# Router product on turned tokens before norm and shift, other bank pairs for two output projections, and fillers in the attentions

## Chip, cores, metric

One core of one Trainium2 chip. The metric is device time of one execution in microseconds (us), median of several.

## What is computed

256 tokens of width 1024 pass two layers and then a second block. Each layer is attention (A: forgetting attention, B: latent attention), output projection with a gate, and a grouped mixture of experts:

```python
x = x + g1[:, None, :] * mix
h = modulate(rmsnorm(x, ffn_norm_g[layer]), sh2, sc2)      # h*(1+sc2)+sh2
x = x + g2[:, None, :] * grouped_moe(h, router_w, router_bias, ...)
# in grouped_moe
scores = sigmoid(hf @ router_w)                            # 16 experts in 4 groups
g = argmax over groups of the sum of the best two (scores + bias)
# the best two experts of that group, weights normed to sum 1
```

The modulation vectors (sh1, sc1, g1, sh2, sc2, g2) come from silu(c) @ w_mod + b_mod. The second block (state space branch, sparse attention, and a product-key expert layer that gathers rows by index) follows.

## The kernel before

All engines run programs written out by hand, with semaphores between them; what stands first in an engine's list runs first. Tokens lie in C=2 chunks of P=128 partitions. PS is the partial-sum memory, 8 banks of 512 columns. TensorE works on a pair of banks for each piece of a matmul stage; `pair_of` says which, and `before[g]` is the last earlier piece on that pair, whose evacuation must be waited for.

The work around the change, in order, for layer 0 (layer 1 is the same with attention B, `b_o`, `mod1_e`):

- `attention("A")`: eight steps. TensorE computes scores two steps ahead (`scores`), VectorE masks them and takes the maximum (`mask`), ScalarE exponentiates (`exps`), VectorE divides (`norm`), TensorE turns them (`transposes`), ScalarE copies them out (`pt`), TensorE multiplies by the values (`values`), ScalarE copies (`o`). Beside it ScalarE and VectorE split the projection's weights into high and low parts (`highs`, `lows`).
- `gemm("a_o")`, the output projection, 96+96 matmuls of 512 columns in split form; VectorE adds gate times result to X (`add_product`, L2113).
- `gemm_mod("mod0_d")`: a piece of the modulation in two partial products (L952) that ScalarE copies to PARTS (L1652), then summed over partitions (`mod_total`, L961). VectorE adds it into MOD (`add_mod`, L2099).
- VectorE computes sum of squares (L2059; ScalarE does the second chunk, L1784), the inverse root by a polynomial (`inverse_root`, six small operations), then for each chunk H = X * root * GAIN (L2074), H = H + shift (L2078), where GAIN already holds norm weight times (1+scale). After each chunk `h_ready` rises.
- `experts(layer)`: TensorE issues fillers (`keep_clock`, L1072, one matmul is two records of 128 columns), turns the chunk of H (L1110) for ScalarE to copy into HT (L1611), and multiplies by the router's weights (L1116). ScalarE: sigmoid (L1711). VectorE: scores, group choice (to L2339), while H is cut into a rounded high part (L2316 on VectorE for chunk 0, L1712 on ScalarE for chunk 1) and the rest, the low part (L2310). TensorE counts group members (L1130 to L1134). VectorE derives the order of groups (`order`, L2360; SP's expert loads wait for it), and the slots as selection matrices PICKS (L2403). TensorE gathers tokens into slots (`slot_rows`, L1151: high and low part, two chunks, 8 banks: 32 matmuls of 384 columns), ScalarE copies them out (L1727), and the quads of expert matmuls begin (L1206, L1221). In layer 0, four strips (L1082) and biases (L1097) of later modulations stand between router and slot rows in TensorE's list, evacuated by ScalarE at L1718.
- SP loads expert weights in a ring of four slots (L723). POOL loads bias rows into GAIN and other accumulators (L784) after `h_ready`. ScalarE computes two Sin (L1830, L1832) before `tp("h_ffn0")`.

## Time and profile before

| | us |
|---|---|
| median of 3 runs | 1844.51 (1844.16 to 1849.18) |
| profiled execution | 1842.19 |
| its span, first to last instruction | 1840.4 |
| TensorE busy | 1668.8 (91%) |
| VectorE busy | 1013.4 (55%) |
| ScalarE busy | 637.6 (35%) |
| mean granted TensorE clock | 0.991 of full |
| HBM read | 606.21 MB, 330 GB/s over the span |

The stages: attention A from about 134 us, its projection to 193, experts of layer 0 from 227 to about 497, attention B from 613, projection to 671, experts of layer 1 from 705 to 975, then the second block, whose gather of rows by index ends the execution. Busy shares are means over stages with different limits; what counts for the change is the chain in the stretch between an output projection and the first expert quad, and at the start of each attention.

### The profile page before, as it was taken

To read this page: it belongs to the slowest core of one execution; us is meant where nothing else is said; L and a number is where in the kernel's file an instruction comes from. 1 tells how busy PE (TensorE), PEld (TensorE's weight loads), DVE (VectorE), ACT (ScalarE), POOL (GpSimd) and SP (SyncE) were. 2 spreads that over 40 slices of the span, in tenths; PEclk is the share of its full clock that TensorE was granted. 3 is DMA by queue.
4 is the path that set the end of the run, shared out by engine and by line. 5 is a ranking of instruction groups with operands and counts; after the bars stand their busy time and mean duration, and the time that the engine had idled before them with its cause. 6 is when DMAs were issued, how large, how long until landed. Compare 5 with 4: busy or idle time off the path is not lost.

```text
span 1840.4 us, 25300 instructions
## 1 busy us (share of the span) xinstructions
PE 1668.8 (91%) x9813; PEld 831.6 (45%) x9813; DVE 1013.4 (55%) x2154; ACT 637.6 (35%) x1162; POOL 303.7 (16%) x342
## 2 busy tenths in 40 slices
PE   8998999999999799999999999999899977777777
PEld 4866633323376575333336554655445533233322
DVE  4327721232473763233237985567776676767655
ACT  2336344434234633544433013322222232222222
POOL 0100000000000000000800000143334353343330
PEclk9999999999999999999999999999999999999999
DMA  9881899999856419999983434499999999999997
GB/s 360 295 301 58 338 418 352 417 416 416 345 205 235 166 46 366 414 400 388 390 329 107 160 136 161 192 425 425 424 419 419 426 427 427 426 428 427 427 427 295
DMA packets 154667, 608.92 MB, mean 331 GB/s; under 512 B 13338, under 2 KB 18626, under 8 KB 121139
## 3 DMA queue, kind: packets, MB, share of 16 engines
q1 hardware_dynamic: 114752, 327.03, 46.1%
q0 software_dynamic: 39504, 279.59, 36.3%
q8 instruction: 77, 1.26, 0.3%
q10 hardware_dynamic: 292, 0.70, 0.1%
q14 instruction: 42, 0.34, 0.0%
HBM read 606.21 MB, written 1.05 MB: 330 GB/s over the span
## 4 chain that ended last, share of the span: by engine, by line
PE 62%; DMA 24%; DVE 8%; ACT 3%; issue 2%; POOL 1%; SPq 0%; ACTq 0%; DVEq 0%; POOLq 0%
PE PS L1221 17%; DMA peer_rows<-in_peer_rows,MOD 15%; PE PS L1206 9%; PE PS L901 6%; PE PS L1594 6%; DMA AR<-in_peer_rows,MOD 5%; PE PS L922 4%; PE PS L1399 2%; PE PS L892 2%; PE PS L952 2%; DVE peer_rows L2889 2%; PE PS L1492 2%; PE PS L1268 1%; PE PS L1553 1%; PE PS L928 1%
## 5 line engine op out<-in xcount | busy, mean ns | idle before, releaser
L1594 PE MATMUL PS<-peer_rows,MOD 128*128 128x512 f32 x756 | 359.3, 614 | 85.3 <-ACT MOD L1985 85.3
L2889 DVE SCALAR_TENSOR_TENSOR peer_rows<-peer_rows,PS 128x1024 f32<-128x1024 f32 x189 | 230.4, 1219 | 139.1 <-DMA peer_rows<-in_peer_rows,MOD 139.1
L1221 PE MATMUL PS<-peer_rows,AR 128*32 128x512 f32 (+1 forms) x1920 | 289.0, 592 | 0.0
L1594 PEld LDWEIGHTS PS<-peer_rows,MOD 128*128 128x128 f32 x756 | 138.2, 193 | 278.8 <-ACT MOD L1985 142.5
L2455 DVE COPY MOD<-peer_rows 128x1024 f32 x96 | 69.5, 724 | 309.0 <-PE PS L1221 104.5
L844 POOL DMA_INDIRECT peer_rows<-in_peer_rows,MOD x189 | 180.5, 955 | 355.8 <-PE PS L1594 262.0
L1221 PE MATMUL PS<-MOD,AR 128*32 128x512 f32 x640 | 225.5, 592 | 0.0
L1985 ACT ACTIVATE MOD<-consts,MOD 128x128 f32<-128x128 f32 x256 | 89.1, 394 | 284.6 <-DVE MOD L2900 284.6
L1221 PEld LDWEIGHTS PS<-peer_rows,AR 128*32 128x32 f32 x1920 | 80.6, 110 | 190.6 <-issue 182.8
L1206 PE MATMUL PS<-peer_rows,AR 128*32 128x512 f32 x1280 | 154.3, 599 | 5.2 <-DMA peer_rows<-in_down_units 2.5
L1736 ACT ACTIVATE MOD<-peer_rows 128x1024 f32 x96 | 96.1, 1050 | 119.1 <-DMA peer_rows<-in_down_units 40.9
L1736 ACT ACTIVATE peer_rows<-peer_rows 128x1024 f32 x96 | 96.2, 1052 | 97.3 <-DMA peer_rows<-in_down_units 40.1
L2203 DVE TENSOR_TENSOR weights_low<-peer_rows,weights_high 128x1024 fp32r<-128x1024 f32 (+1 forms) x57 | 66.9, 1186 | 79.0 <-ACT weights_high L1620 78.6
L1594 PE MATMUL PS<-AR,MOD 128*128 128x512 f32 x184 | 86.5, 600 | 18.2 <-ACT MOD L1985 18.2
L1979 ACT ACTIVATE MOD<-MOD 128x2 f32<-128x2 f32 (+1 forms) x131 | 26.6, 203 | 190.8 <-DVE peer_rows L2889 121.9
L1620 ACT ACTIVATE weights_high<-peer_rows 128x1024 fp32r<-128x1024 f32 (+1 forms) x57 | 57.9, 1029 | 96.5 <-PE PS L901 55.7
L1206 PEld LDWEIGHTS PS<-peer_rows,AR 128*32 128x32 f32 x1280 | 39.7, 110 | 94.2 <-issue 86.7
L2889 DVE SCALAR_TENSOR_TENSOR AR<-AR,PS 128x1024 f32<-128x1024 f32 x46 | 56.1, 1220 | 35.1 <-DMA AR<-in_peer_rows,MOD 35.1
L901 PE MATMUL PS<-weights_high,tokens_high 128*128 128x512 f32 (+1 forms) x164 | 64.3, 392 | 4.9 <-ACT AR L1806 3.2
L1594 PEld LDWEIGHTS PS<-AR,MOD 128*128 128x128 f32 x184 | 33.8, 191 | 67.3 <-issue 36.4
L901 PE MATMUL PS<-weights_high,tokens_low 128*128 128x512 f32 (+1 forms) x164 | 63.0, 384 | 0.0
L901 PE MATMUL PS<-weights_low,tokens_high 128*128 128x512 f32 (+1 forms) x164 | 62.9, 384 | 0.0
(434 smaller groups left out, 2589.5 us busy)
## 6 DMA issues: line engine op xcount, KB each, us to landing
peer_rows<-in_exp_w_gate SPq DMA_DIRECT2D x128, 512.0 KB, 7.6
peer_rows<-in_exp_w_up SPq DMA_DIRECT2D x128, 512.0 KB, 8.0
peer_rows<-in_down_units SPq DMA_DIRECT2D x128, 512.0 KB, 7.7
peer_rows<-in_w_mod SPq DMA_DIRECT2D x20, 2048.0 KB, 9.2
peer_rows<-in_a_w_in SPq DMA_DIRECT2D x6, 2048.0 KB, 10.0
peer_rows<-in_w_in SPq DMA_DIRECT2D x5, 2048.0 KB, 7.7
peer_rows<-in_kv_w_mod SPq DMA_DIRECT2D x16, 512.0 KB, 8.2
peer_rows<-in_w_mod SPq DMA_DIRECT2D x16, 512.0 KB, 8.0
```

The lines of the kernel that those rows point to most:

```text
L844: pool.indirect_dma_start(out=pair_row(k), out_offset=None, in_=A["peer_rows"], in_offset=bass.IndirectOffsetOnAxis(ap=EXPERT[:, c, PT_ * ...
L901: last = nc.tensor.matmul(PS[:, pair + c, 0:n], tokens[b][:, 2 * j + k, P * c:P * c + P], ws[a][:, k, :], start=j == 0 and k == 0 and i == ...
L922: last = nc.tensor.matmul(PS[:, pair + c, 0:n], lhs[:, k, P * c:P * c + P], w[:, k, off:off + n], start=k == 0, stop=k == s["kb"] - 1)
L1206: nc.tensor.matmul(PS[QUARTER * i:QUARTER * i + QUARTER, banks, :], left[:, 0, at + k, QUARTER * i:QUARTER * i + QUARTER], raw(slot, 0)[:, ...
L1221: last = [nc.tensor.matmul(PS[QUARTER * i:QUARTER * i + QUARTER, banks + tile, :], left[:, tile, at + k, QUARTER * i:QUARTER * i + QUARTER ...
L1594: last = nc.tensor.matmul(PS[:, 4 + 2 * c + half, :], diagonal(k), v_row(k)[:, 512 * half:512 * half + 512], start=k == 0, stop=j == SEL - 1)
L1620: A_(high, src, ACT.Copy).then_inc(S("cut_high"), 1)
L1736: A_(copy_of(n, 1 + i), routed(ring_slot(layer, "E", n), choice, 0, UW), ACT.Copy).then_inc(S("moe_copy_a"), 1)
L1985: A_(diagonal(k), ident, ACT.Copy, scale=WEIGHT[:, n, j:j + 1]).then_inc(S("diagonals"), 1)
L2203: V.tensor_tensor(low, src, high.bitcast(fp32), ALU.subtract).then_inc(S("cut_low"), 1)
L2455: V.tensor_copy(copy_of(n, 0), routed(ring_slot(layer, "E", n), choice, 0, UW)).then_inc(S("moe_copy_d"), 1)
L2889: V.scalar_tensor_tensor(u_row(k), u_row(k), 1.0, PS[:, 2 * c:2 * c + 2, :].rearrange("p a k -> p (a k)"), ALU.mult, ALU.mult, accum_out=D ...
```

## The change

The router's product is linear, so with s = shift and r = inverse root it is computed as r * ((X * GAIN) @ rw) + s @ rw. TensorE turns X * GAIN, without norm and shift; VectorE applies root and the shift's product to the 16 sums of each token before the sigmoid. The shift's product is made at the start of each attention: `shift_columns` turns the shift row into columns, eight matmuls with one row and one column moved, ScalarE copies them, `shift_logits` multiplies by the router's weights, eight matmuls of 16 columns, and ScalarE copies again. The full H is made after turning. Both conversions to high parts are ScalarE's, both low parts stand on VectorE after the picks. The modulation piece's totals move behind the router on TensorE, its adding behind the group choice on VectorE, the wait for it before the slot rows. Slot rows go in four groups instead of pairs. Sin moves behind the conversions. The output projections use pairs 0 and 2, `mod0_d` and `mod1_e` pairs 0 and 6. Fillers: 6, 2, 4, 4 around turning and router (before 15, 2, 3, 2), 14 for 8 ahead of the group sums in layer 1, none between strips in layer 0, and 6 and 8 at the start of the attentions. A semaphore pair is merged (f_abs into logf), with no change of order.

```diff
+    for name in ("mod0_d", "mod1_e"):
+        pair_of[stages[name][0][0]], pair_of[stages[name][1][0]] = 0, 6
+    for name in ("a_o", "b_o"):
+        pair_of[stages[name][0][0]], pair_of[stages[name][1][0]] = 0, 2
...
-        pool.wait_ge(S("h_ready"), C * h_no["ffn0"])
+        pool.wait_ge(S("h_full"), C)
...
+            def shift_columns():
+                for k in range(DB):
+                    last = nc.tensor.matmul(PS[:, 7, k:k + 1], MOD[0:1, 3 * D + P * k:3 * D + P * k + P], ones[0:1, 0:1],
+                                            start=True, stop=True)
+                last.then_inc(S("shift"), 1)
+            def shift_logits():
+                pe.wait_ge(S("shift"), 4 * (a == "B") + 2)
+                for k in range(DB):
+                    last = nc.tensor.matmul(PS[:, 7, 2 * NE:3 * NE], SHIFT_T[:, k:k + 1].to_broadcast((P, P)), rw[:, k, :],
+                                            start=k == 0, stop=k == DB - 1)
+                last.then_inc(S("shift"), 1)
             scores(0)
             scores(1)
+            shift_columns()
+            stay_busy(6, 5)
             for n in range(len(steps)):
                 if n + 2 < len(steps):
                     scores(n + 2)
+                if n == 0:
+                    shift_logits()
+                    stay_busy(8, 5)
                 if n >= 1:
                     values(n - 1)
...
+            mods = stages[("mod0_d", "mod1_e")[layer]]
+            for piece in mods:
+                mod_partial(*piece)
-            keep_clock(15, 2)
-            for c in range(C):
+            def turn(c):
                 pe.wait_ge(S("h_ready"), C * (h_no[f"ffn{layer}"] - 1) + c + 1)
...
+                    if n == first + 1:
+                        pe.wait_ge(S("mod_copied"), mod_no[mods[1][0]] + 1)
...
+            keep_clock(6, 1)
+            turn(0)
+            keep_clock(2, 1)
+            turn(1)
+            keep_clock(4, 1)
+            router(0)
+            keep_clock(4, 1)
+            router(1).then_inc(S("router_mm"), 1)
+            for piece in mods:
+                mod_total(*piece)
             if layer == 0:
                 mod_strips(0)
             else:
-                keep_clock(8)
+                keep_clock(14, 5)
...
             pe.wait_ge(S("picks"), C * layer + 1)
-            pe.wait_ge(S("h_split"), C * layer + 1)
+            pe.wait_ge(S("h_high"), C * layer + 1)
             for b in (0, 1, 6, 7, 2, 3, 4, 5):
...
-                for x in range(2):
-                    slot_rows(0, x, b)
+                slot_rows(0, 0, b)
             pe.wait_ge(S("picks"), C * layer + 2)
-            pe.wait_ge(S("h_high"), layer + 1)
+            pe.wait_ge(S("h_high"), C * layer + 2)
             for b in range(DB):
                 slot_rows(1, 0, b)
+            pe.wait_ge(S("h_split"), C * layer + 1)
+            for b in range(DB):
+                slot_rows(0, 1, b)
             pe.wait_ge(S("h_split"), C * layer + 2)
             for b in range(DB):
                 slot_rows(1, 1, b).then_inc(S("slots_mm"), 1)
...
         # ScalarE, attention
+            act.wait_ge(S("shift"), shifts + 1)
+            A_(SHIFT_T[:, :], PS[:, 7, 0:DB], ACT.Copy).then_inc(S("shift"), 1)
             for n in range(N + 2):
                 if n < N:
                     exps(n)
+                if n == 0:
+                    act.wait_ge(S("shift"), shifts + 3)
+                    A_(SHIFT_ROW[:, :], PS[:, 7, 2 * NE:3 * NE], ACT.Copy).then_inc(S("shift"), 1)
...
         # VectorE, experts
+            for c in range(C):
+                V.tensor_tensor(H[:, c, :], X[:, c, :], GAIN[:, :], ALU.mult).then_inc(S("h_ready"), 1)
...
+            L(V.scalar_tensor_tensor(HTL[:, 0:4, :].rearrange("p b t -> p (b t)"), X[:, 0, :], 1.0, X[:, 0, :],
+                                     ALU.mult, ALU.mult, accum_out=st[:, 0:1]))
+            wait("square", square_no[("a_o", "b_o")[layer]])
+            ts(st[:, 2:4], st[:, 0:2], 1.0 / D, ALU.mult, EPS, ALU.add)
+            inverse_root(st[:, 2:4])
+            for c in range(C):
+                wait("tp_done", TPJ[f"h_{ffn}"][0] + 2 * c + 2)
+                V.scalar_tensor_tensor(H[:, c, :], H[:, c, :], root(c), shift, ALU.mult, ALU.add).then_inc(S("h_full"), 1)
+            wait("shift", 4 * layer + 4)
+            wait("router_mm", layer + 1)
+            for c in range(C):
+                last = V.scalar_tensor_tensor(RSC[:, c, :], PS[:, 0, NE * c:NE * c + NE], root(c), SHIFT_ROW[:, :],
+                                              ALU.mult, ALU.add)
...
-            h_low(0, DB // 2, DB)
+            add_mod(*(("mod0_d", MOD0["mod0_d"]), ("mod1_e", MOD1["mod1_e"][0]))[layer])
...
             V.tensor_copy(CHOICE_I, CHOICE).then_inc(S("choice"), 1)
-            wait("h_high", layer + 1)
+            h_low(0)
             h_low(1)
```

## Rows read from the trace of the kernel before

**Rows 1.** Page, part 4: shares of the chain, by engine.

```profile
PE 62%; DMA 24%; DVE 8%; ACT 3%; issue 2%; POOL 1%; SPq 0%; ACTq 0%; DVEq 0%; POOLq 0%
```

**Rows 2.** Chain, layer 0: start us, us, what.

```profile
192.79 3.57 PE PS L952 x32
196.35 1.92 PE PS L961 x4
198.27 3.35 PE PS L1072 x30
201.62 0.87 PE PS L1110 x8
...
206.78 1.78 PE PS L1116 x16
...
217.39 1.87 PE PS L1082 x16
...
220.90 4.35 PE PS L1151 x25
...
226.67 1.92 PE PS L1206 x16
```

**Rows 3.** Timeline, VectorE, layer 0: start us, us, line, tiles [idle before].

```profile
195.41 1.22 DVE L2059 SCALAR_TENSOR_TENSOR H<-X 128x1024 f32<-128x1024 f32 x1
...
197.92 1.28 DVE L2074 SCALAR_TENSOR_TENSOR H<-X,roots,GAIN 128x1024 f32<-128x1024 f32 x1
199.24 1.23 DVE L2078 TENSOR_TENSOR H<-H,MOD 128x1024 f32<-128x1024 f32 x1
...
208.81 0.19 DVE L2013 TENSOR_TENSOR AR<-AR,rb 128x32 f32<-128x32 f32 x1 [1.65 <-ACT AR L1711]
...
219.10 1.03 DVE L2403 TENSOR_TENSOR picks<-consts,AR 128x384 fp32r<-128x384 f32 x2
...
220.12 2.11 DVE L2310 TENSOR_TENSOR tokens_low<-H,tokens_high 128x1024 fp32r<-128x1024 f32 x1
```

**Rows 4.** Timeline, TensorE, layer 0.

```profile
211.09 0.39 PE L1130 MATMUL PS<-AR,consts 128*128 128x4 f32 x2 [0.67 <-DVE AR L2339]
```

**Rows 5.** Timeline, ScalarE, attention A and layer 0.

```profile
141.36 0.51 ACT L1669 ACTIVATE AR<-AR,st 128x256 f32<-128x256 f32 x1 [1.08 <-DVE st L2174]
...
208.68 2.15 ACT L1712 ACTIVATE tokens_high<-H 128x1024 fp32r<-128x1024 f32 x1
220.38 1.03 ACT L1718 ACTIVATE GAIN<-PS 128x1024 f32<-128x1024 f32 x1 [9.56 <-PE PS L1097]
```

**Rows 6.** Timeline, TensorE, layer 1.

```profile
688.94 0.39 PE L1130 MATMUL PS<-AR,consts 128*128 128x4 f32 x2 [0.65 <-DVE AR L2339]
...
697.59 0.69 PE L1151 MATMUL PS<-picks,tokens_high 128*128 128x384 f32 x1 [2.35 <-DVE picks L2403]
```

**Rows 7.** Windows: us, busy PE, PEld, DVE, ACT, POOL; clock, DMA share, GB/s.

```profile
144.00:148.00 4.00, 3.84 (x46) 2.96 (x44) 3.97 (x4) 4.00 (x12) 0.00 (x0) 1.00 0.00 0
208.00:210.00 2.00, 2.00 (x21) 0.92 (x20) 1.02 (x6) 1.74 (x3) 0.00 (x0) 1.00 1.03 418
300.00:380.00 80.00, 79.97 (x744) 24.31 (x736) 17.45 (x22) 35.41 (x37) 0.00 (x0) 1.00 1.02 405
698.00:700.00 2.00, 2.00 (x8) 2.00 (x8) 2.00 (x3) 0.00 (x0) 0.00 (x0) 0.50 0.95 256
```

**Rows 8.** Timeline, VectorE, layer 1.

```profile
702.11 0.69 DVE L2455 COPY MOD<-peer_rows 128x1024 f32 x1 [2.10 <-DMA peer_rows<-in_exp_w_gate]
```

**Rows 9.** Timeline, TensorE, starts of attentions A and B.

```profile
138.64 0.39 PE L999 MATMUL PS<-AR 64*128 64x128 f32 x4
...
142.20 0.66 PE L1016 MATMUL PS<-consts,AR 128*128 128x128 f32 x4 [2.50 <-DVE AR L2184]
...
620.07 0.66 PE L1016 MATMUL PS<-consts,AR 128*128 128x128 f32 x4 [2.49 <-DVE AR L2184]
```

**Rows 10.** Waits of TensorE, 226 to 500: total, times, longest.

```profile
PE PS L1206 <- DMA peer_rows<-in_down_units: 2.5, 1, 2.5
```

More of the change, by code:

```diff
@@ L184, in build @@
     ROOT = sb("roots", [P, 2, ROOTS, ROOT_TERMS])
+    SHIFT_T = sb("shift_turned", [P, DB])
+    SHIFT_ROW = sb("shift_logits", [P, NE])
     PS = ctx.enter_context(nc.psum_tensor("PS", [P, 8, 512], fp32))
@@ L1111, in experts, with router @@
                     last.then_inc(S("tp_done"), 1)
-                keep_clock(2, 2)
+            def router(c):
                 for k in range(DB):
@@ L1360, in _ @@
         gemm("b_o", None)
-        gemm_mod("mod1_e")
         experts(1)
@@ L1689, in attention @@
                 return exps, pt, o
+            shifts = 4 * (a == "B")
+            act.wait_ge(S("shift"), shifts + 1)
+            A_(SHIFT_T[:, :], PS[:, 7, 0:DB], ACT.Copy).then_inc(S("shift"), 1)
             N = len(steps)
@@ L2306, in experts @@
         def experts(layer, beside=iter(())):
-            HN = [x[:, :, :].rearrange("p b t -> p (b t)").rearrange("p (c b q) -> p c b q", c=C, b=DB)
-                  for x in (HTH, HTL)]
-            def h_low(c, first=0, end=DB):
-                last = V.tensor_tensor(HN[1][:, c, first:end, :],
-                                       H[:, c, :].rearrange("p (q b) -> p b q", b=DB)[:, first:end, :],
-                                       HN[0][:, c, first:end, :].bitcast(fp32), ALU.subtract)
-                if end == DB:
-                    last.then_inc(S("h_split"), 1)
@@ L2316, in experts @@
-            L(V.tensor_copy(HN[0][:, 0, :, :], H[:, 0, :].rearrange("p (q b) -> p b q", b=DB)))
-            h_low(0, 0, DB // 2)
-            wait("router_sig", layer + 1)
+            ffn, shift = f"ffn{layer}", mod_part(3)
+            wait_gain(ffn)
+            for c in range(C):
+                V.tensor_tensor(H[:, c, :], X[:, c, :], GAIN[:, :], ALU.mult).then_inc(S("h_ready"), 1)
+                counts["h_ready"] += 1
+            wait("h_ready", counts["h_ready"])
+            dve.sem_inc(S("gain_used"), 1)
@@ new lines, in experts, with h_low @@
+            wait("shift", 4 * layer + 4)
+            wait("router_mm", layer + 1)
+            for c in range(C):
+                last = V.scalar_tensor_tensor(RSC[:, c, :], PS[:, 0, NE * c:NE * c + NE], root(c), SHIFT_ROW[:, :],
+                                              ALU.mult, ALU.add)
+            last.then_inc(S("router_scores"), 1)
+            def h_low(c):
+                HN = [x[:, :, :].rearrange("p b t -> p (b t)").rearrange("p (c b q) -> p c b q", c=C, b=DB) for x in (HTH, HTL)]
+                wait("h_high", C * layer + c + 1)
+                V.tensor_tensor(HN[1][:, c, :, :], H[:, c, :].rearrange("p (q b) -> p b q", b=DB),
+                                HN[0][:, c, :, :].bitcast(fp32), ALU.subtract).then_inc(S("h_split"), 1)
@@ L2320, in experts @@
+            wait("router_scores", 2 * layer + 2)
             tt(RSEL, RSC, rb[:, :].rearrange("p (a e) -> p a e", a=1).to_broadcast((P, C, NE)), ALU.add)
@@ L2396, in experts @@
             L(V.tensor_reduce(best, of_token.rearrange("p c g m -> p c (g m)"), AX.X, ALU.add))
-            V.tensor_tensor(SLOT, SLOT, best, ALU.add).then_inc(S("slots"), 1)
-            wait("slots", layer + 1)
+            L(V.tensor_tensor(SLOT, SLOT, best, ALU.add))
             tt(SLOTM, SLOT.rearrange("p (c a) -> p c a", a=1).to_broadcast((P, C, TILES)),
@@ L2605, in _ @@
         add_product("a_o", mod_part(2))
-        rms(X, D, H, "ffn0", shift=mod_part(3), signal="h_ready", squared="a_o")
-        add_mod0("mod0_d")
         experts(0)
@@ L2657, in _ @@
         add_product("b_o", mod_part(2))
-        rms(X, D, H, "ffn1", shift=mod_part(3), signal="h_ready", squared="b_o")
-        add_mod1("mod1_e")
         experts(1, beside=ssm_parameters())
```

43 lines of the change are left out of this document (20 added, 23 removed).

## The prediction, as put on record before the changed kernel was run

> **What bounds the kernel now.** I read the page's chain first, then the chain in order of time around the first expert layer, then each engine's timeline there, then the same stretches of the second layer and the starts of attentions A and B. The page gives 62% of the chain to TensorE and 24% to DMA [rows 1]. All of the change lies ahead of the experts, so what counts is how late a step there pushes the first expert quad; nothing behind it has a fixed time, and the rest shifts with it.
>
> In layer 0 the chain runs through TensorE without a gap from the end of the output projection (192.8) to the router's last matmul: two modulation partials 3.57, totals 1.92, fillers 3.35 for 30 records (0.112 each), turning at 0.87 a chunk, and the router at 1.78 for 16 records (0.11 each), done at 208.56. Then come sigmoid, group choice on VectorE, strips, slot rows, and the first quad at 226.67 [rows 2]. VectorE had X ready at 195.41 and the shifted first chunk at 200.47, a little before TensorE came to it; it starts on the scores at 208.81 and writes the picks from 219.10 [rows 3]. Between them TensorE waits 0.67 for the group choice [rows 4].
>
> **The FFN stretch, layer 0.** Times here are those of the kernel before, with the attention's delay added at the end. Partials end at 196.3 as before. Totals (1.92) leave this place, and fillers here shrink from 30 to 12 records (1.34): 197.65. The turned thing is now X times GAIN, one 1.23 us product per chunk from 195.41: ready 196.65 and 197.8, so no wait. The root chain, 1.3 long (196.6 to 197.92) [rows 3], and the 1.28 and 1.23 of norm and shift leave TensorE's path. Turning 0.87, fillers 0.45, turning 0.87, fillers 0.9, router 1.76, fillers 0.9, router 1.76 end at 205.15, drained 205.3, against 208.56: 3.25 earlier. VectorE meanwhile does both products, square, root, and both full rows (1.28 each), done about 203, under the router. Added on the path are two small VectorE operations on the 16 sums and a hop, 0.4 (one of VectorE's small operations takes 0.19 [rows 3]). Scores start about 205.95 instead of 208.81: 2.85 earlier; the group choice is ready at 208.2.
>
> Now TensorE is late: the two totals (1.92) have moved here, then strips 0 (1.87, the price of 16 records) [rows 2], so the group sums start at 208.95, not 211.09 [rows 4]: 2.1 earlier. VectorE's two modulation sums (1.3) fit under that. The picks follow 2.1 earlier, at 217.0, and the first is done at 217.5. Three sets of strips (5.6) and the biases (1.0) follow the group sums (1.1) without their fillers and end near 216.7, so TensorE, in whose row of the chain the slot rows stand at 220.90 though the first picks were done by 219.65, is no longer late for them. What is late next is VectorE: both subtractions of the high parts now stand after the picks, and the one there took 2.11 from 220.12 to 222.2 [rows 3]. Two of them, begun at 218.1 and overlapping by a tenth, end at 222.2, as the last did before. TensorE runs three groups of eight slot rows at 0.174 (4.2 from 217.5, plus up to 0.5 for the bank copies) and is ready for the last group at about 222.2 too. Its first record ends 222.6 rather than 225.25: **2.6 earlier**. ScalarE hides the two conversions (2.15 each, from 206 to 210.2) and Sin with its table ahead of the bank copies at 216.8 [rows 5]. SP's expert loads need the order and a released strip slot, both 2.1 earlier; POOL's bias loads wait for h_full at 203, some 2.5 later than for h_ready, but are used only at 216. Bounds: 3.25 if the picks and conversions don't hold it, 0 if data does (rival 2). Other bank pairs remove no wait in the chain: zero, the cover being that both partials already ran back to back.
>
> **The FFN stretch, layer 1.** The router again ends 3.25 earlier. This layer's stretch lies 477.85 later (688.94 against 211.09) [rows 4, 6]. Behind the router stand totals (1.92) and 14 fillers, 28 records (3.14), 5.05 together, where VectorE needs 2.9 to the group choice. Before, TensorE waited 0.65 for it; now the group sums start at 205.15+477.85+5.05=688.05, only 0.9 earlier. The following 22 fillers are the same, so TensorE idles about as long before the picks as before: 2.35, after which the granted clock was 0.50 (the lower of the two levels) [rows 6, 7]. I take the same dip for the first slot rows. They start 0.85 earlier, and as the groups no longer wait for conversions between them I round to **1.0 earlier**. Without a dip VectorE's subtractions set the start of the last group: they end 0.9 before 222.2+477.85, at 701.2, and the gain is about 2. The first expert unit lands 0.85 earlier than 702.11, where VectorE waited for it [rows 8], and does not bind.
>
> **The attentions.** This is where the forecast is decided. Ahead of the loop come shift_columns and 6 fillers; after scores(2), shift_logits and 8 fillers. Eight matmuls are 16 records, as in the router, so 1.76 + 1.34 + 1.76 + 1.79 = 6.65 us of TensorE. In A scores(2) ran from 138.64, then TensorE stood idle 2.50 until the first transposes at 142.20; in B the idle time is 2.49 [rows 9]. So transposes(0) is 6.65 - 2.50 = 4.15 later. Worse, ScalarE waits in its queue for the logits between exps(0) and exps(1), and behind it VectorE's norm(1) and all copies of turned probabilities. exps(1) began at 141.36 [rows 5]; now 138.64+1.76+1.34+0.9+1.76 ends 144.4, with drain and copy 144.75: 3.4 later. The first high part then comes behind the later pt(0), and VectorE's subtraction and mask(3) follow 3.6 later. That isn't won back: between 144 and 148 VectorE is busy 3.97 of 4 us and ScalarE 4.00 [rows 7]. I take 3.6 for each attention, **7.2 later** in all; bounds 0 (some slack later swallows it) and 4.15 each.
>
> No row shows a matmul of one row and one column. The nearest are the router's 16-column ones at 0.11, the same as fillers of 128 columns, so the weights' 128 columns look like the price; that is the value I take.
> The Trainium skill, page "TensorE: Matmul & The Clock Gate", section "Wait — 56ns, not 53.3ns?", gives a floor of about 25 ns between starts however few columns move; by that alone each set of 16 would cost 0.4 (an estimate from that page) and an attention 1.4 rather than 4.15, near rival 1. The same page's "Step-by-step: what each phase is for" says that weight loading scales with the columns of the array, which speaks for the trace's 0.11.
>
> **Sum.** 7.2 - 2.6 - 1.0 = +3.6. The profiled execution took 1842.19 (span 1840.4): 1845.8 for a like one, span 1844.0. The median before, 1844.51, lies 2.3 above it; 1844.51+3.6 = **1848.1**.
>
> **Rivals.** (1) One-column matmuls are cheap. If the two sets cost next to nothing, TensorE still adds 6.65-3.52-2.50=0.63 per attention; halfway to a third of the router's price it is about 1.0, which I take. Sum 2.0-3.6 = -1.6: 1842.9. Against it: the 0.11 of the router and the group sums.
> (2) Data takes the place of TensorE in layer 0, and the case is slower. DMA is saturated at 418 GB/s from 200 on [rows 7] and the first loads don't start earlier relative to the projection, so the expert units still land when they did and their lead over TensorE shrinks by the 2.6 won. It decides if that lead isn't built up again to what the four slots allow before the modulation units come between. For it: TensorE already stood 2.5 at once for a down unit [rows 10]. Against: from 300 to 380 only 405 GB/s were drawn, a 4% reserve, which refills the lead. Price: the 2.6 is lost, and with a filler late or another dip 1 more: +6.2 to +7.2, 1850.7 to 1851.7.
> (3) The attentions hide all of it, because their tails wait on each other and not on busy engines: -3.6, 1840.9, and -4.65 or more with no dip in layer 1 (at most -6.5, the router's 3.25 twice). Against: the 3.97 of 4.
> (4) The change doesn't shorten anything, because fillers replace what the root leaves: +7.2, within rival 2's numbers.
>
> **How the numbers follow.** Forecast 0.58; rival 1 0.14; rivals 2 and 4 together 0.16; rival 3 0.12. About what a measurement can tell from no change is 0.3%, 5.5 us. Slower beyond it: rivals 2 and 4, 0.16, and 0.03 of the forecast's upper tail: 0.19. Faster beyond it: the outer part of rival 3, 0.06. Same: 0.75. The range takes in rivals 1 and 2 and the inner part of 3: 1841 to 1853; the attention's upper bound (+1.1) lies inside it.
>
> **What would show it.** In the profile after: transposes(0) of A some 4 us after scores(2) ends with TensorE full between, and exps(1) waiting for TensorE, right; if the two small matmul sets take under 0.6 each, rival 1. The distance from the projection's end to the router's last matmul should fall from 15.8 to 12.5, to the first quad from 33.9 to 31.3 in layer 0, and the same distance in layer 1 by 1.0. If TensorE waits on expert units early in layer 0, rival 2; if the output projections start at the same time, rival 3. The dip at 698 staying or going moves layer 1 by 1.05. What would make it wrong is mostly the attention term, the only one above 3.

## The result and the profile after

The changed kernel took 1850.71 us (median of 20 runs, 1847.33 to 1859.81) against 1844.89 for the kernel before (20 runs, 1842.38 to 1852.18). The ratio is 1.004, 95% interval 1.0029 to 1.0050: slower, by about the 0.3% that the prediction took as its bound or a little more (5.8 us between the medians, 7.1 between the means). The forecast was 1848.1, and the range 1841 to 1853 holds the time; "within 0.3%" was its likeliest case, and the time lies just outside it, in the case that it had given 0.19. The profiled execution of the changed kernel (1858.26, span 1856.5) is among its slowest; its mean granted clock is 0.987, while its five fastest runs had 0.989 to 0.992. This profile has to be read with the clock beside it.

Cutting the spans at the same points gives this table; "after, run again" is the profile of the first experiment below. A starts with attention A's first scores, the next cut is the output projection's first matmul, then the first modulation partial, then the first expert quad.

| stretch, us | before | after | after, run again | forecast of the difference |
|---|---|---|---|---|
| start to A's first scores | 135.91 | 136.34 | 137.77 | 0 |
| A: scores to projection | 33.63 | 37.85 | 37.85 | +3.6 |
| projection to partials | 23.18 | 23.16 | 23.17 | 0 |
| layer 0: partials to router's end | 15.83 | 12.76 | 12.63 | -3.25 |
| layer 0: partials to group sums | 18.37 | 17.94 | 16.25 | -2.1 |
| layer 0: partials to first quad | 33.95 | 33.19 | 31.88 | -2.6 |
| first quad to B's first scores | 387.12 | 389.47 | 386.33 | 0 |
| B: scores to projection | 33.61 | 41.96 | 37.44 | +3.6 |
| layer 1: partials to group sums | 18.36 | 19.11 | 20.73 | -0.9 |
| layer 1: partials to first quad | 34.57 | 34.25 | 36.82 | -1.0 |
| rest | 1135.25 | 1137.14 | 1135.49 | 0 |

The first row lies ahead of all that the change moves, and in the later profiles, with other edits, it is 136.1 to 137.6: 1 to 2 us between two single profiles of such a long stretch can't be put down to an edit.

Attention A, the timeline of TensorE in the changed kernel (start us, us, line, tiles, records, idle before), answers to [rows 9]:

```profile
139.16 1.94 PE L1047 MATMUL PS<-consts,MOD 1*128 1x1 f32 x16
141.03 1.60 PE L879 MATMUL PS<-consts 128*128 128x128 f32 x12
...
143.66 1.96 PE L1055 MATMUL PS<-rw,shift_turned 128*128 128x16 f32 x16
145.47 2.03 PE L879 MATMUL PS<-consts 128*128 128x128 f32 x16
147.34 0.60 PE L1022 MATMUL PS<-consts,AR 128*128 128x128 f32 x4
```

The same stretch on ScalarE, which answers to the first row of [rows 5]:

```profile
141.14 0.18 ACT L1733 ACTIVATE shift_turned<-PS 128x8 f32<-128x8 f32 x1 [4.90 <-PE PS L1047]
141.34 1.28 ACT L1710 ACT_TABLE_LOAD   x1
142.63 0.40 ACT L1710 ACTIVATE AR<-AR,st 128x128 f32<-128x128 f32 x1
...
145.66 0.18 ACT L1740 ACTIVATE shift_logits<-PS 128x16 f32<-128x16 f32 x1 [1.38 <-PE PS L1055]
145.74 0.50 ACT L1710 ACTIVATE AR<-AR,st 128x256 f32<-128x256 f32 x1
```

TensorE is full up to the first transposes, which come 5.14 later than before (4.7 with the start's 0.43 taken off). A matmul of one row and one column takes what one of 128 columns takes: 1.94 for 16 records. The second exps (145.74, before 141.36) wait for the copy of the logits, and that waits for TensorE.

Layer 0, TensorE in the changed kernel; it answers to [rows 2, 4]:

```profile
208.13 1.98 PE L1150 MATMUL PS<-rw,HT 128*128 128x16 f32 x16
209.95 3.53 PE L967 MATMUL PS<-mod_parts,consts 128*128 128x512 f32 x4
...
215.29 0.39 PE L1171 MATMUL PS<-AR,consts 128*128 128x4 f32 x2
...
223.98 3.06 PE L1191 MATMUL PS<-picks,tokens_high 128*128 128x384 f32 x16 [1.08 <-issue]
226.89 1.55 PE L1191 MATMUL PS<-picks,tokens_low 128*128 128x384 f32 x8
228.66 1.69 PE L1191 MATMUL PS<-picks,tokens_low 128*128 128x384 f32 x8 [0.22 <-DVE tokens_low L2382]
230.54 1.92 PE L1248 MATMUL PS<-peer_rows,AR 128*32 128x512 f32 x16 [0.19 <-ACT AR L1780]
```

And VectorE there, answering to [rows 3]:

```profile
223.32 1.03 DVE L2468 TENSOR_TENSOR picks<-consts,AR 128x384 fp32r<-128x384 f32 x2
...
224.34 4.26 DVE L2382 TENSOR_TENSOR tokens_low<-H,tokens_high 128x1024 fp32r<-128x1024 f32 x2
```

The router ends early, as forecast, but the two totals behind it took 3.53 instead of 1.92. The windows (us, busy PE, clock, DMA share, GB/s; the same view as [rows 7], for TensorE alone) tell why, and show the same in attention B and layer 1:

```profile
204.00:208.00 4.00, 4.00 (x38) 1.00 1.02 410
208.00:214.00 6.00, 6.00 (x31) 0.72 1.03 415
...
625.00:630.00 5.00, 5.00 (x31) 0.61 0.12 47
630.00:637.00 7.00, 7.00 (x31) 0.54 0.00 0
...
698.00:702.00 4.00, 4.00 (x13) 0.60 0.01 4
```

In each of them the granted clock was at its lower level, 1.2 GHz, for a while, and TensorE had been busy without a gap for the 5 us before and during it. In B the price is plain:

```profile
622.83 1.94 PE L1047 MATMUL PS<-consts,MOD 1*128 1x1 f32 x16
...
627.83 3.43 PE L1055 MATMUL PS<-rw,shift_turned 128*128 128x16 f32 x16
631.11 3.76 PE L879 MATMUL PS<-consts 128*128 128x128 f32 x16
634.66 1.06 PE L1022 MATMUL PS<-consts,AR 128*128 128x128 f32 x4
```

Logits and fillers took 7.2 where A needed 4.0 for the same records. In the kernel before the clock was at full speed in these stretches of layer 0 and B. Layer 1, TensorE, answering to [rows 6]:

```profile
697.60 3.56 PE L967 MATMUL PS<-mod_parts,consts 128*128 128x512 f32 x4
700.95 3.44 PE L1098 MATMUL PS<-consts 128*128 128x128 f32 x28
704.22 0.28 PE L1171 MATMUL PS<-AR,consts 128*128 128x4 f32 x2
...
712.80 3.04 PE L1191 MATMUL PS<-picks,tokens_high 128*128 128x384 f32 x16 [2.39 <-issue]
...
719.36 1.92 PE L1248 MATMUL PS<-peer_rows,AR 128*32 128x512 f32 x16 [0.20 <-ACT AR L1780]
```

The dip that the kernel before had on its first slot rows is gone (16 of them in 3.04), and another stands ahead of the group sums. In the experts, where [rows 10] had 2.5 for a down unit, TensorE's waits for DMA (total, times, longest) are:

```profile
PE PS L1248 <- DMA peer_rows<-in_down_units: 3.9, 1, 3.9
PE PS L1248 <- DMA peer_rows<-in_exp_w_gate: 2.3, 2, 1.5
```

### The profile page after: what moved, and what is told of

Its sections match the earlier page's. It is cut to its first block, busy times and chain, and to the rows that moved or that the text cites. A ratio compares the mean times of both kernels' runs of the same rounds, so it can differ in the third digit from the quotient of the medians.

```text
span 1856.5 us, 25503 instructions
## 1 busy us (share of the span) xinstructions
PE 1687.0 (91%) x9909; PEld 846.1 (46%) x9909; DVE 1012.2 (55%) x2154; ACT 642.0 (35%) x1168; POOL 302.5 (16%) x342
## 3 DMA queue, kind: packets, MB, share of 16 engines
q8 instruction: 78, 1.28, 0.3%
## 4 chain that ended last, share of the span: by engine, by line
PE 61%; DMA 24%; DVE 8%; ACT 3%; issue 2%; POOL 1%; SPq 0%; ACTq 0%; DVEq 0%; POOLq 0%
PE PS L1263 17%; DMA peer_rows<-in_peer_rows,MOD 15%; PE PS L1248 9%; PE PS L907 6%; DMA AR<-in_peer_rows,MOD 5%; PE PS L1635 5%; PE PS L928 4%; PE PS L1440 2%; PE PS L898 2%; PE PS L958 2%; DVE peer_rows L2950 2%; PE PS L1533 2%; PE PS L967 1%; PE PS L1310 1%; PE PS L934 1%
```

## The experiments

Two theories were set against each other. Theory 1: each stretch costs the length and order of its work. Theory 2: what goes beyond that is granted clock, lost behind matmuls that move few columns. "Before" is each time the kernel before on the same chip.

**The changed kernel again** (no edit).

> The changed kernel once more, on the chip of the next three. Theory 1 (work put at the start of each attention costs its length, with ScalarE's table load behind the first copy): the stage distances are the same in every execution, output projection of A 4.2 us later than before. Theory 2 (narrow matmuls let the granted clock fall, and where it falls differs from one execution to the next): the stretches at 0.50 lie elsewhere than in the first profile (625 to 636 in attention B, 209 to 213 in layer 0), and attention B costs 4 us in a profile without a fall there and over 8 with one. Time 1847 to 1859.

Measured: 1854.31 (1850.07 to 1857.94), before 1845.01; ratio 1.0055 (1.0039 to 1.0071). Attention B was at full clock throughout (same windows as above) and took 37.44 instead of 41.96:

```profile
625.00:630.00 5.00, 5.00 (x38) 1.00 0.00 0
630.00:637.00 7.00, 6.29 (x60) 1.00 0.01 2
```

and layer 0 reached its group sums after 16.25, the forecast's 2.1 early. But in layer 1 the clock was at half from 690 to 696, with TensorE busy, and again from 707 to 710, behind an idle time of 2.39, and the first quad came 2.25 late instead of 1.0 early:

```profile
690.00:692.00 2.00, 2.00 (x5) 0.50 0.03 8
```

Its layer 0 also shows a wait that the profile of the first execution hides, at the fourth set of strips (timeline of TensorE):

```profile
220.59 1.95 PE L1108 MATMUL PS<-peer_rows,cT 128*32 128x512 f32 x16 [0.67 <-DMA peer_rows<-in_kv_w_mod]
```

Here the last group of slot rows no longer waited for VectorE: behind the late strips ScalarE's copies of their banks ended at 225.61, and the slot rows for those banks started at 225.65. So the places of the clock's falls change from one execution to the next, while A, and projection to partials, which had none, agree within 0.01 us.

**The attentions' part alone**, on the kernel before; run twice:

```
+            shift_columns()
+            stay_busy(6, 5)
             for n in range(len(steps)):
                 if n + 2 < len(steps):
                     scores(n + 2)
+                if n == 0:
+                    shift_logits()
+                    stay_busy(8, 5)
```

> The kernel before with only the attention part of the change: shift columns, shift logits, 6 and 8 fillers and the two copies, whose result nothing uses. Theory 1: each attention 4.2 longer, nothing else moves, so 8.4 later in all, 1853. Theory 2: as much or more, with a fall of the clock in attention B in some executions, 1853 to 1861. Rival 3 of the prediction (attentions hide it): within 1 us of before.

> The variant with the attentions' part of the change alone, again, on one chip with its wide form. Theory 1 (cost by length and order; the runs' spread is chance): its time is 6.5 to 8.5 us above the kernel before, and the wide form's is the same within 1 us. Theory 2 (narrow matmuls let the clock fall): it is 8 to 10 us above, its runs spread over 6 us or more, and half-clock time stands within 15 us after the first scores of one attention.

Measured: 1854.61, before 1845.01, ratio 1.0062 (1.0044 to 1.0079), and 1854.45, before 1844.34, ratio 1.0052 (1.0033 to 1.0071). A took 37.84 and 37.86, B 39.06 and 39.07, with half clock from 623 to 627 in both profiles. The attentions' part costs 9.6 to 10.1, where 7.2 was forecast; of that, 4.2 in A and 3.6 to 3.8 in B is length at full clock (B's from the run above and from the next two, which have other matmuls in these places), and 1.6 is B's fall.

**The same with wide matmuls**: eight and eight matmuls of 128 columns, ones times the unit matrix, in the places of the narrow ones; the shift isn't computed. Run twice (the loop alone is shown):

```
+                for _ in range(DB):
+                    last = nc.tensor.matmul(PS[:, 7, 0:P], ones, ident, start=True, stop=True)
```

> The kernel before with its router as it was, and in each attention eight plus eight matmuls of 128 columns (constants times the unit matrix) where the changed kernel has its eight column turns of one column and eight logit matmuls of 16 columns; fillers, waits and ScalarE's two copies as in the changed kernel. The shift is not computed for the router, which takes its tokens as before. Theory 1 (cost by length and order): the sets take 1.9 us each again (8 x 2 x 0.11), each attention is 37.85 to 38.0 from first scores to projection, and the time is that of the variant with the narrow ones, 1852 to 1855. Theory 2 (the clock falls behind matmuls of few columns): no half clock within 15 us after the first scores of either attention, both attentions under 38.0 (the narrow variant had 39.06 in B, the changed kernel 41.96 and 37.44), total half-clock time 31 us as before, and the time 1 to 2 us under the narrow variant.

> The same variant with 8 and 8 matmuls of 128 columns in place of the narrow ones, again, on one chip with the narrow form. Theory 1: within 1 us of the narrow form. Theory 2: 6.5 to 7.5 us above the kernel before, so 1.5 or more under the narrow form, its runs within 3 us of one another, and no half clock within 15 us after the first scores of either attention.

Measured: 1853.11 (1851.49 to 1854.38), before 1846.31, ratio 1.0036 (1.0024 to 1.0047), and 1850.57, before 1844.34, ratio 1.0035 (1.0020 to 1.0049). A took 37.75 and 37.77, B 37.16 and 37.17: the same work at the same length, with no half clock in either attention. This is the same view as for B above:

```profile
620.00:625.00 5.00, 5.00 (x41) 1.00 0.82 317
625.00:630.00 5.00, 5.00 (x45) 1.00 0.02 5
```

The wide form cost 6.2 to 6.8, the narrow one 9.6 to 10.1, at lengths that are equal within 0.3 at full clock. That speaks for theory 2, though the intervals of the ratios overlap (1.0033 to 1.0079 against 1.0020 to 1.0049), and B's fall in the narrow profiles explains 1.6 to 1.9 of the 2.8 to 3.9 between the two.

**The changed kernel without the attentions' fillers** (both `stay_busy` lines out).

> The changed kernel without the 6 and 8 fillers at the start of the attentions. Theory 1: scores(2) come 1.34 earlier, the first transposes 3.1 earlier; ScalarE's second exponentials 1.34 earlier; so 1.3 to 1.5 less per attention, 3 us less in all: 1848. Theory 2: the clock falls more often, or at least in attention B, and half of it or more is given back: 1850 or more.

Measured: 1853.27, before 1845.01, ratio 1.0043 (1.0027 to 1.0058). A fell only to 36.94 though 28 records, 3.6 us, were gone from TensorE: the engine then stood idle for 1.19 ahead of the first transposes, and the clock was at half from 145 to 149. B took 38.56, again with a fall. The time came out as theory 2 said (1850 or more, where theory 1 had 1848): taking the fillers out gave back 1.0 of 9.3 us against the changed kernel on the same chip, which the intervals don't separate from nothing. What fillers cost at full clock is not shown by this run. Its layer 0 is worth a look too, since its attentions were still late: TensorE waited longer for weights than in the changed kernel run again, and the first quad came after 36.67, 2.7 late:

```profile
220.32 3.52 PE L1106 MATMUL PS<-peer_rows,cT 128*32 128x512 f32 x16 [2.25 <-DMA peer_rows<-in_kv_w_mod]
```

**Exp's table ahead of the wait**, on the changed kernel:

```
             shifts = 4 * (a == "B")
+            A_(SHIFT_ROW[:, 0:1], ones[:, 0:1], ACT.Exp)
             act.wait_ge(S("shift"), shifts + 1)
```

> The changed kernel with one Exp of a single column on ScalarE ahead of its first wait for the turned shift, so that the table load for Exp (1.28 us, in the changed kernel at 141.34, right ahead of the first exps) runs while ScalarE waits. Nothing is left out. Theory 1 (the table load stands in the chain: first copy, table, first exps, second copy): the first exps start at 141.3 to 141.5 counted as in the changed kernel, 1.2 us earlier, and each attention is 0.6 to 1.3 shorter than 37.85 from first scores to projection, the time about 2 us less than the changed kernel. Rival (the second exps wait for the copy of the logits at 145.7, which waits for TensorE's eight logit matmuls, and these bind): the first exps are earlier, the second ones are not, attention stays within 0.3 us of 37.85 and the time within 1 us.

Measured: 1850.88, before 1846.31, ratio 1.0034 (1.0017 to 1.0052). ScalarE's timeline in A:

```profile
136.38 1.28 ACT L1732 ACT_TABLE_LOAD   x1
...
141.34 0.39 ACT L1710 ACTIVATE AR<-AR,st 128x128 f32<-128x128 f32 x1
...
145.86 0.50 ACT L1710 ACTIVATE AR<-AR,st 128x256 f32<-128x256 f32 x1
```

The first exps come 1.3 earlier, the second ones not, and A took 37.84. The rival stated there was right: the table load looked like a new cost in the profile after, but the logits set the time. Layer 0 had half clock from 210 to 214 again, and B from 623 to 627. Layer 1 had full clock ahead of its first quad, and reached its group sums in 17.41 (0.95 early) and the quad in 32.47 (2.1 early).

**The shift's work at the attentions' ends**, on the changed kernel. A first form (`late_shift`: columns after the third transposes from the end, logits after the next, sums still in bank 7) was expected at 1842 to 1846 and gave no time: nothing in it ordered ScalarE's reading of that bank behind TensorE's writing. Here the work lies in halves, the sums are in banks 0 and 1 with waits of their own, ScalarE's two copies move behind its last copies of the attention, and the attentions' fillers are gone (the loop on TensorE alone is shown):

```
-            shift_columns()
-            stay_busy(6, 5)
...
-                if n == 0:
-                    shift_logits()
-                    stay_busy(8, 5)
...
                 transposes(n)
+                if n == len(steps) - 3:
+                    shift_columns(0, 4)
+                if n == len(steps) - 2:
+                    shift_columns(4, DB)
+                if n == len(steps) - 1:
+                    shift_logits(0, 4)
             values(len(steps) - 1)
+            shift_logits(4, DB)
```

> The changed kernel with the shift's turning and its logits moved from the starts of the two attentions to their ends: eight column matmuls in two halves of four after the transposes of the last steps but two and but one, eight logit matmuls in two halves after the last transposes and after the last values, no fillers among them, and ScalarE's two copies behind its last probability copies. Everything is computed that the changed kernel computes. Theory 1 (the length of the shift's work at the attention's start, and ScalarE's copies ahead of the first exps, are what attention costs): each attention is within 1.5 us of the kernel before from its first scores to the output projection (33.6, where the changed kernel has 37.85), the feed-forward part keeps its 31.9 to 33.2 us from partials to first quad in layer 0 against 33.95, and the time is 1841 to 1846, about 7 us under the changed kernel. Theory 2 (what the change costs is granted clock lost behind matmuls of few columns, wherever they stand): the distances in the attentions are the same as theory 1 says only where the clock stays at 1.00, the half-clock stretches stay as many as in the changed kernel (48 to 56 us of span against 31), and the time is 1848 or more.

Measured: 1847.99 (1843.07 to 1852.30), before 1846.31, ratio 1.0008 (0.9995 to 1.0021). From A's first scores to the partials it is 56.95 against 56.81 before, so the same sums, made in the last steps and without fillers, cost 0.1 rather than 4.2 with them (3.3 in the run without fillers, which had a fall in A). But the 4 us that the FFN stretches should then bring didn't come, and the time lies above theory 1's 1841 to 1846. In layer 0 TensorE ran into data:

```profile
216.58 1.95 PE L1115 MATMUL PS<-peer_rows,cT 128*32 128x512 f32 x16 [1.20 <-DMA peer_rows<-in_kv_w_mod]
...
227.21 1.92 PE L1255 MATMUL PS<-peer_rows,AR 128*32 128x512 f32 x16 [0.78 <-DMA peer_rows<-in_exp_w_gate]
```

(first quad 32.97 after the partials, 0.98 early, with DMA at a share of 1.01 or more from 205 on); in B and layer 1 the clock fell. No narrow matmul stands at B's start here, so theory 2 as it was stated isn't the whole of it (windows and timeline of TensorE):

```profile
620.00:625.00 5.00, 3.96 (x12) 0.57 0.07 27
...
621.04 1.11 PE L1022 MATMUL PS<-consts,AR 128*128 128x128 f32 x4 [2.49 <-DVE AR L2242]
```

But this fall is of another kind than B's falls above: TensorE stood idle for 2.49 just ahead of it, as it did in the kernel before, where [rows 9] has the same 2.49 and no fall came. B's falls in the two of the next runs that have one came behind the same idle time.

**That, with the FFN part reordered**: the first total ahead of the turning, the second between the router's sets, ScalarE's first conversion ahead of the sigmoid, VectorE's modulation sums ahead of the scores, and half of the first subtraction behind the group choice.

```
-            keep_clock(6, 1)
+            mod_total(*mods[0])
             turn(0)
...
             router(0)
-            keep_clock(4, 1)
+            pe.wait_ge(S("tp_out"), first + 3)
+            mod_total(*mods[1])
             router(1).then_inc(S("router_mm"), 1)
-            for piece in mods:
-                mod_total(*piece)
```

> The variant with the shift's work at the attentions' ends, and its feed-forward part reordered: the total of the first modulation piece ahead of the first turning in place of six fillers, that of the second between the two router sets (instead of both behind the router), two fillers twice as long between the turnings, 12 for 14 fillers in layer 1; ScalarE converts the first tokens ahead of the sigmoid; VectorE adds the modulation ahead of the router's scores, and splits half of the first low part behind the group choice. Everything is computed. Theory 1 (after the change, what sets the first quad is VectorE's chain with the two low parts at its end): partials to first quad falls to 29 to 30.5 us in layer 0 (33.95 before, 31.9 to 33.2 in the changed kernel) and by 2 to 4 in layer 1, and the time is 1837 to 1842, the best of all. Rival (TensorE waits for DMA in the experts' first part whatever the order): the distances fall but the stretch from first quad to attention B's scores grows by the same, 387.1 to 389 and more, and the time is that of the variant without the reordering within 1.5 us.

Measured: 1843.91 (1840.16 to 1851.06), before 1846.31, ratio 0.9984 (0.9971 to 0.9997). The expectation was 1837 to 1842. In layer 1 the quad came after 31.11, 3.5 early. In layer 0 the group sums came 3.4 early (14.95) and the quad 3.1 late (37.07): TensorE waited 2.37 for in_kv_w_mod, and the clock fell three times between 210 and 227.

**Reordered in layer 1 alone** (`if layer == 0:` the changed kernel's order, else the new one).

> The variant with the shift's work at the attentions' ends, its feed-forward part in the changed kernel's order in layer 0 and in the reordered one in layer 1. Everything is computed. What it tells apart: in layer 0 the reordering brought its group sums 1.3 us forward and its first quad 4.1 us back, with 2.4 us of TensorE waiting for the weights in_kv_w_mod and the clock at half from 210 to 227; in layer 1, which has no such weights to wait for, it brought the first quad to 31.1 from 34.6. Theory (layer 0 is bound by data, so an earlier router only turns TensorE's work into waits for DMA; layer 1 is bound by VectorE's chain): partials to first quad 32.5 to 33.5 in layer 0 with a wait for DMA ahead of the last strips or the first quad, 30.5 to 31.5 in layer 1, B's first scores within 1 us of 614.8, and the time 4 to 6 us under the kernel before of the same chip. Rival (the 4.1 us were chance, a clock fall that comes and goes): the time is that of the fully reordered variant, 2.4 us under the kernel before, within 1 us.

Measured: 1843.49 (1836.50 to 1846.26), before 1844.34, ratio 0.9988 (0.9974 to 1.0001). I had expected 4 to 6 us under the kernel before and 32.5 to 33.5 to the quad in layer 0. The reordering is not needed for the loss there: with the changed kernel's order, which had given 32.97 in the profile of the run before the reordering, the quad now took 37.78 (timeline of TensorE):

```profile
218.35 3.67 PE L1115 MATMUL PS<-peer_rows,cT 128*32 128x512 f32 x16 [3.17 <-DMA peer_rows<-in_kv_w_mod]
...
223.80 5.02 PE L1209 MATMUL PS<-picks,tokens_high 128*128 128x384 f32 x16
```

Sixteen strips took 3.67 instead of 1.95 and sixteen slot rows 5.02 instead of 3.06, behind a longer wait for the same weights. With layer 0 the same in both programs, 4.8 us lie between two profiles, so one profile each can't rank orders of layer 0.

**That, with the router's matmuls 128 columns wide** (the first of each set 256), the wanted chunk always landing on the same 16 columns, which VectorE reads:

```
+ at, wide = 256 * c + P - NE * k, rw[:, :, :].rearrange("p (a k) e -> p a (k e)", a=1)
+ last = nc.tensor.matmul(PS[:, 0, at:at + P] if k else PS[:, 0, 256 * c:256 * c + 256],
+          HT[:, k, P * c:P * c + P], wide[:, 0, :] if k else wide.to_broadcast((P, 2, P)),
```

> The variant before it, with the router's matmuls 128 columns wide (the first of each token tile 256): every one multiplies by all 8 chunks of the router's weights, its output laid so that the chunk that is wanted falls on the same 16 columns each time; the other columns are not read. As many matmuls and as many weight loads as with 16 columns. Everything is computed. Theory 1 (a matmul of 16 columns costs what one of 128 costs, and the columns do nothing to the clock): the router's two sets take 1.9 to 2.0 us each as with 16 columns, and the time is within 1 us of the narrow form. Theory 2 (after a stretch of narrow matmuls the granted clock falls): no half clock from 5 us ahead of the group sums to 5 us behind them in either layer (the changed kernel's layer 0 had 3.4 us of it there, in layer 1 its two totals took 3.4 instead of 1.9), and the time is 1 to 3 us less than the narrow form, with less spread between its runs.

Measured: 1842.51 (1838.67 to 1844.79), before 1844.34, ratio 0.9984 (0.9973 to 0.9996). No fall ahead of the group sums or in B; the one behind the data wait in layer 0 stayed (quad at 37.01). The runs' spread is 6.1 instead of 9.8, but the medians differ by 1.0 only, within both intervals. The second set of 16 records took 2.15 instead of 1.86. It is 0.16% faster than the kernel before on the same chip, as the reordered run was: the gain in length is there, and small. It was run on another chip than the changed kernel.

**Fillers in the wait for data**: `keep_clock(16, 0)` between the third and the fourth set of strips in layer 0.

> The variant with the wide router matmuls, with 16 filler matmuls of 128 columns (1.8 us at 0.11) in layer 0 between the third and the fourth set of strips, where TensorE sat idle for 2.2 us for the weights in_kv_w_mod, and the clock was at half for the stretch behind it (the fourth set took 3.62 instead of 1.94, ten slot rows 3.40 instead of 2.0). Everything is computed. Theory (the clock falls behind TensorE's wait for data): the fourth set starts at the same distance from the partials (23.7) and takes 1.95, the distance to the first quad falls from 37.0 to 33 to 34 in layer 0, and the time is 2 to 4 us less than the variant's (1838 to 1841 where the kernel before takes 1844.3). Rival (the fall comes for another reason, as it did in the changed kernel ahead of the strips with no idle time at all): half clock stays within that stretch, the distance stays above 35, and the time is within 1 us of the variant's.

Measured: 1843.81, before 1845.39, ratio 0.9991 (0.9982 to 1.0000). TensorE's timeline:

```profile
214.57 3.84 PE L1105 MATMUL PS<-consts 128*128 128x128 f32 x32
218.34 1.94 PE L1115 MATMUL PS<-peer_rows,cT 128*32 128x512 f32 x16
...
223.40 3.51 PE L1212 MATMUL PS<-picks,tokens_high 128*128 128x384 f32 x10 [0.30 <-ACT AR L1794]
```

Sixteen fillers are 32 records, so they took 3.84, not the 1.8 that my expectation said; they filled the wait and 1.5 more. The strips then ran at full speed, but ten slot rows took 3.51 instead of 2.0: the fall came later, with pauses of 0.3 ahead and no long idle time. The rival's case. I can't say from these runs what sets the place of a fall.

**What all fourteen profiles say of the falls.** From 120 us on, leaving out the end of the execution, twelve falls began with no pause of TensorE over 0.1 us in the 5 us before. Each of the twelve began while a set of matmuls that move 1 or 16 columns ran, or at most 1.4 after it: five in B, behind the columns' turning (after, both runs of the attentions' part, without fillers, table ahead), and seven at the router (after twice, and once each in run again, without fillers, table ahead, at the ends, and reordered in layer 1 alone). Every other fall had an idle time of over 1 us in those 5 us, but for four in layer 0's slot rows, which had pauses of 0.3. With wide matmuls in the same places, no such fall stands in the two profiles of the attentions' wide form or the two with the wide router. That is more for narrow matmuls than the run times gave. It doesn't make them enough: the same narrow sets passed at full clock in A in five of six profiles, and at the router in the kernel before's order in all five.

## Why the prediction was right, and where not

**The attentions: right in kind, 0.6 short in A.** Forecast 3.6 each; at full clock A measured 4.2 and B 3.6 to 3.8. The steps held: one-column matmuls at the price of the router's (0.12 a record; rival 1 is refuted), TensorE full, transposes(0) 4.7 later (4.15 forecast), exps(1) behind the logits and 3.95 later than before with the start's 0.43 off (3.4 forecast). What was short are small terms: the four sets take 7.1 from start to start (1.87, 1.54, 1.81, 1.87), not 6.65, and ScalarE's copy starts only behind the last record's end (145.66 for the logits that end at 145.62, where TensorE had gone on at 145.47). Rival 3, that the attentions' tails hide the delay, is refuted: both projections started later by the full amount.

**Layer 0: right, with a floor that I had put among the rivals.** Router's end 12.63 to 12.76 against 12.5; group sums 2.1 early, exactly as worked out; first quad 2.07 early at full clock against 2.6. What is late next was named correctly for the first profile (the two subtractions, 4.26 from 224.34, with TensorE waiting 0.22 for them ahead of the last slot rows); in the second, at full clock, it was the strips and the copies of their banks, behind a wait for in_kv_w_mod (0.67); as far as this profile shows, the missing 0.5 lies there. That is the floor, and the attentions' delay hides it only in part: TensorE waited 2.25 there in the run without fillers, with the attentions late, and 1.20 to 3.17 in four runs with them early. The mechanism of rival 2 is thus real, but not at its place (the expert units) nor at its price: TensorE's waits for expert weights in layer 0 sum to 3.8 to 6.2 in the four profiles with the changed kernel's FFN and attentions (with and without fillers, and with the table moved), and to 4.8 in the kernel before and 5.6 with the attentions' part alone, whose down unit was waited for 3.4, so the 3.9 after is no sign of it. (Its reserve of 405 under 418 GB/s is 3%, not 4%.) The stretch from first quad to B is 386.33 to 389.47 in those four, on the mean 1.6 above the 385.59 to 387.12 of the five profiles with the kernel before's FFN. The half clock in it, 3.4 to 6.8 us against 0 to 3.4, can account for that: half of the time at half clock is lost where TensorE is busy (an estimate). Rival 4 is refuted: the router ends 3.1 to 3.2 earlier.

**Layer 1: right in the lengths, and the dip decided.** Group sums 0.95 early (0.9 forecast); the first quad 2.1 early in the one profile of this order with no fall, which is the prediction's "Without a dip [...] the gain is about 2". (Its working there says that the subtractions end 0.9 before 222.2+477.85, which would be 699.2, and then 701.2; only 701.2 follows from its other numbers.) I had taken the dip as fixed in its place. In the changed kernel it moved to the totals and fillers, where it cost more: 0.3 early in one profile and 2.25 late in another.

**The sum.** At full clock 4.2 + 3.8 - 2.1 - 2.1 = +3.8, against +3.6 forecast. That the sum is so near is luck: the attentions were 0.8 short and layer 0 0.5 too good, layer 1 1.1 too poor. The medians differ by 5.8, the means by 7.1, which leaves 2.0 to 3.3 for what the sum lacked. Clock fits it: the mean clock of the changed kernel's 20 runs is 0.9877, and of the kernel before 0.9892 to 0.9901 over the four groups of 12 to 33 runs that were made beside the experiments (its 20 runs beside the changed kernel have no clock on record). A difference of 0.0015 to 0.0024 over 1848 us is 2.8 to 4.4 us of full-speed time, which costs up to that where TensorE is on the path (an estimate from these means). I had priced clock only where the kernel before showed it; no run measures those 2.0 to 3.3 by themselves.

The Trainium skill, page "TensorE: Matmul & The Clock Gate", section "HAM oscillation — how this bites in real kernels", describes falls behind waits for DMA. The runs show that case (3.67 us for 16 strips behind a wait of 3.17) and also falls that this section doesn't describe, in B at 5.00 busy of 5.00. The 25 ns floor for few columns of the Trainium skill's same page, section "Wait — 56ns, not 53.3ns?", which the prediction had set beside the trace, isn't reached by weights of 128 columns: 1.94 us for 16.

## What to carry to other kernels

Work that is added at the start of a pipelined stage can cost nearly its whole length less the idle time there; here 7.1 less 2.5 cost 4.2. The shift's work cost those 4.2 us at the attention's start, with its fillers, and 0.1 in its last steps, where it had none. A step that is taken off a path is worth only what the next floor leaves, so look for the transfer that would be late next before shortening an engine's work. Where an engine's clock can fall, cost a change by several profiles at equal stages and give the clock a term of its own, on both sides.

## What the runs showed of the hardware

- The granted clock fell to half while TensorE was busy without a gap (clock 0.61 and 0.54 over 12 us in B). The places differ between executions of one kernel: B at 626 to 636 in one, layer 1 at 690 to 696 in the other.
- With 128-column matmuls in place of narrow ones, two profiles of two had no fall in the attentions, against falls in B in five of the six profiles with the narrow ones at its start. All twelve falls without a pause ahead began at narrow matmuls, but most sets of narrow matmuls passed without one, and falls behind idle time of TensorE came without any near. That narrow matmuls are the cause is likely by this, and not proven.
- ScalarE's table load for Exp (1.28) goes to the first place where Exp is next in its queue: at 135.88, hidden, in the kernel before; at 141.34, behind the wait, when a copy with a wait stands ahead; at 136.38, hidden, when a one-column Exp comes before that wait.
